# The place of six groups: a pass of two and then one of four, instead of four and then two

## The reference

```python
logits = (hf @ w_router + b_router)
top_val, top_idx = lax.top_k(logits, TOP_K)
gates = jax.nn.softmax(top_val, axis=-1)
# for each expert e and the tokens xb that chose it:
gu = xb @ w1[e] + b1[e]
gate, up = jnp.split(gu, 2, axis=-1)
gate = jnp.minimum(gate, 7.0); up = jnp.clip(up, -7.0, 7.0)
glu = gate * jax.nn.sigmoid(1.702 * gate)
y = ((up + 1.0) * glu) @ w2[e] + b2[e]
# each token sums its four y, weighted by its gates
```

## The kernel before

| loads | what | slots | free after |
|---|---|---|---|
| 56 to 63 | place 2, up chunks | 8 to 15 | earlier passes |
| 64 to 67 | place 19, down chunks | 0 to 3 | earlier passes |
| 68 to 71 | place 2, down chunks | 4 to 7 | earlier passes |
| 72 to 79 | place 20, up chunks | 8 to 15 | use of load 56 to 63 in up 6, one by one |
| 80 to 83 | place 21, up chunks 0 to 3 | 0 to 3 | down 4 |
| 84 to 87 | place 21, up chunks 4 to 7 | 4 to 7 | use of load 68 to 71 in down 6, one by one |
| 88 to 91 | place 20, down chunks | 8 to 11 | up 7 |

## Time and profile before

### The profile page before, as it was taken

How to read it: one execution, slowest core, us unless ns; L and a number is a source line. 1 busy time by engine, 2 the same in 40 slices (tenths; PEclk the granted TensorE clock), 3 DMA queues, 4 the chain that set the end, 5 groups by cost and what they waited for, 6 DMA issues and landing times.

```text
span 2083.2 us, 36376 instructions
## 1 busy us (share of the span) xinstructions
PE 1999.2 (96%) x15871; PEld 900.5 (43%) x15871; DVE 630.7 (30%) x1256; ACT 404.9 (19%) x837; POOL 53.6 (3%) x54
## 2 busy tenths in 40 slices
PE   8999897999999999999999999879999999999998
PEld 4455444433443343443443433455444444444443
DVE  5979765211111111111111110143444444300002
ACT  3223402110111010111110110113333443300001
POOL 0000000000000000000000000030000000000000
PEclk9999997999999999999999999989999999999999
DMA  8753686999899999999999999960222112122201
GB/s 325 264 212 132 240 314 268 420 419 359 327 420 420 420 418 421 419 420 420 419 420 420 419 420 419 395 242 11 104 66 74 63 64 69 57 81 71 81 32 70
DMA packets 109169, 553.82 MB, mean 266 GB/s; under 512 B 14864, under 2 KB 26128, under 8 KB 59216
## 3 DMA queue, kind: packets, MB, share of 16 engines
q1 hardware_dynamic: 87392, 517.36, 61.7%
q10 hardware_dynamic: 14560, 17.29, 2.5%
q0 software_dynamic: 7056, 16.79, 2.2%
HBM read 532.91 MB, written 26.35 MB: 268 GB/s over the span
## 4 chain that ended last, share of the span: by engine, by line
PE 69%; DMA 14%; SPq 9%; DVE 5%; issue 1%; ACT 1%; POOL 0%; ACTq 0%; DVEq 0%; POOLq 0%
PE psum L880 19%; PE psum L1058 13%; PE psum L1065 11%; SPq L417 9%; PE psum L888 8%; DMA arena<-in_w 6%; PE psum L556 4%; DMA ring<-in_w 3%; PE psum L1016 3%; PE psum L1128 3%; DMA ring<-in_dot_slabs 1%; PE psum L874 1%; DMA arena<-in_mod_slabs 1%; DMA ring<-in_mod_slabs 1%; PE psum L1106 1%
## 5 line engine op out<-in xcount | busy, mean ns | idle before, releaser
L880 PE MATMUL psum<-arena,ring 128*32 128x512 f32 x4096 | 451.7, 595 | 12.3 <-DMA arena<-in_w 11.8
L1058 PE MATMUL psum<-h_t,ring 128*128 128x512 f32 x640 | 278.6, 592 | 0.2 <-ACT arena L1432 0.2
L880 PEld LDWEIGHTS psum<-arena,ring 128*32 128x32 f32 x4096 | 133.2, 110 | 326.5 <-issue 324.0
L888 PE MATMUL psum<-arena,h_t 128*32 128x256 f32 x3840 | 213.8, 380 | 5.4 <-DMA arena<-in_w 4.6
L1957 DVE TENSOR_SCALAR h_t<-psum 128x512 f32<-128x512 f32 (+2 forms) x33 | 27.9, 845 | 608.2 <-PE psum L880 608.2
L1359 ACT ACTIVATE ring<-psum,mods,gain 128x64 f32<-128x64 f32 (+2 forms) x264 | 85.8, 430 | 641.9 <-PE psum L866 641.9
L1058 PEld LDWEIGHTS psum<-h_t,ring 128*128 128x128 f32 x640 | 120.4, 190 | 146.4 <-issue 145.9
L888 PEld LDWEIGHTS psum<-arena,h_t 128*32 128x32 f32 x3840 | 123.5, 110 | 87.5 <-DMA arena<-in_w 7.5
L880 PE MATMUL psum<-ring 128*32 128x512 f32 x1344 | 149.0, 593 | 7.8 <-DMA ring<-in_w 7.8
L556 PE MATMUL psum<-h_t,ring 128*128 128x512 f32 x256 | 118.8, 619 | 2.6 <-ACT h_t L1179 2.6
L1065 PE MATMUL psum<-h_t,ring 128*128 128x512 f32 x256 | 112.6, 592 | 1.4 <-ACT work L1243 1.4
(11 more groups left out here) (436 smaller groups left out, 1726.0 us busy)
## 6 DMA issues: line engine op xcount, KB each, us to landing
arena<-in_w SPq DMA_DIRECT2D x288, 1024.0 KB, 27.8
ring<-in_w SPq DMA_DIRECT2D x96, 1024.0 KB, 29.3
ring<-in_dot_slabs SPq DMA_DIRECT2D x40, 512.0 KB, 5.7
ring<-in_turn_slabs SPq DMA_DIRECT2D x40, 512.0 KB, 3.3
ring<-in_merge_slabs SPq DMA_DIRECT2D x32, 512.0 KB, 3.3
ring<-in_mod_slabs SPq DMA_DIRECT2D x6, 2048.0 KB, 13.2
ring<-in_proj_slabs SPq DMA_DIRECT2D x24, 512.0 KB, 4.1
y_rows<-arena SPq DMA_DIRECT2D x3, 3584.0 KB, 19.0
```

What stands on the lines that cost most here:

```text
L880: mm = pe.matmul(psum[32 * j:32 * j + 32, g, :], x_e[:, c * tokens + g * TG:c * tokens + g * TG + TG], slot[s][:, j * S:(j + 1) * S], star ...
L888: mm = pe.matmul(psum[32 * j:32 * j + 32, 6 + g // 2, (g % 2) * 256:(g % 2) * 256 + 256], h_e[:, g * 256 + half * P + 32 * c:g * 256 + hal ...
L1058: mm = pe.matmul(psum[:, bank, :], ring[:, s, k, :], h_t[:, k, :], start=(k == 0), stop=(k == KT - 1))
```

## The change

The list of passes is written differently. A place of up to four groups is one pass, as before. A larger one is first a pass with what is over four groups, and then one of four. Only place 2 has more than four groups, so pass 5 now has two groups and pass 6 four. Everything that is computed from `PASSES` follows: the first group of each pass, the table by which tokens find their rows, and `AT_GROUP`, by which the tokens of a pass of two groups lie in rows 64 to 127 of the gathered tile. The plan of loads, slots and counts is the same in every entry, since both passes use all 12 chunks in either order.

```diff
-PASSES = [(w, at, min(4, GROUPS_OF[w] - 4 * at)) for w in PLACES for at in range(-(-GROUPS_OF[w] // 4))]
+
+PASSES = [(w, at, n) for w in PLACES for at, n in enumerate([GROUPS_OF[w]] if GROUPS_OF[w] <= 4 else [GROUPS_OF[w] - 4, 4])]
```

## The result

The changed kernel takes 2089.16 us (median of 12 runs, 2085.11 to 2095.16), the kernel before 2083.21 (12 runs, 2077.55 to 2085.93). The ratio is 1.0029 with a 95% interval of 1.0019 to 1.0040. That is 6.0 us slower, 4.0 to 8.3. The forecast was 4.5 slower, with a range of 3.2 to 6.0.

A forecast was written before the change was run, and what follows sets the result against it. The weight stream was taken as the bound, restarting after the second hole: 3.8 us for load 91's later landing, 0.4 gather and 0.3 start sum to 4.5 slower, 2086.7; forecast range 3.2 to 6.0 us, whole range 2083.5 to 2090.

The forecast's parts named there:

- What bounds the stage: Mixture of experts: the weight stream bounds it; its end is the second hole's end plus a fixed amount of transfer.
- the second hole: Stretch from 544 to 552 with DMA share 0.02; load 84 has no slot until down 6 uses its first chunk.
- Steps 1 to 3: Up 5 and down 4 follow the loads, then transposes and bias; up 6 starts at 499.1, against 505.75 before.
- the gather's price: Pass 8's earlier gather may delay loads 66 and 67 by up to 0.8 us; half, 0.4, counted after step 2.
- Steps 4 to 6: Up 6 to down 6: down 6 starts at 551.0, load 84 is issued at 554.8, 2.4 us later.
- Behind load 84: Loads 84 to 87 issued 3.49 us apart, a store moved behind the hole; load 91 lands at 581.9, 3.8 later.
- the row of four loads behind load 87: Loads 88 to 91 follow load 87's landing at 570.4 at 2.48 us each, to 580.3, before the store's price.
- TensorE makes good its delay: After down 6 TensorE is 7.6 us late, the stream 4.5; the 3.1 between is gone by 676 through shorter waits.
- The clock: Rival, chance 0.04: TensorE's clock falls after waits from 468 to 497.5; end at 2114, or 2088.7 if only for 4 us.
- The spacing costs nothing: Rival, chance 0.12: the 3.49 us spacing behind the hole hides in slow first loads; only 2.4 us remain, 2084.6.
- The earlier refill counts: Rival, chance 0.04: load 72, issued 4.9 us earlier, keeps the queue from running dry before load 84; faster, 2081.1.
- The DMA price: Skill formula, 2.0 us fixed plus bytes at 436 GB/s: 4.4 us per load; the sum would be 3.8.

The follow-up runs named there:

- delays ahead and behind: Kernel before with nine idle TensorE products ahead of down 6: ratio 1.0029, 6.0 us slower; behind down 6: 0.9989, 2.3 us faster.
- the filled holes: Loads with free slots issued ahead of waiting ones; second hole only, against the kernel before: ratio 0.9957 with its passes, 0.9980 with the changed passes.
- the kernel with the spacing alone: Kernel before with two idle TensorE products ahead of each of the last three chunks of down 6: ratio 1.0016, 3.3 us slower.
- both holes filled: Loads reordered 80 to 83, 72 to 79, 88 to 95, 84 to 87, against the kernel before: ratio 0.9924 with its passes, 0.9938 with the changed passes.
- four and two: Passes 5 and 6 with four and then two groups, as in the kernel before; with the order of loads for both holes: ratio 0.9924, 2067.68 us.
- two and four: Passes 5 and 6 as in the changed kernel; with the order of loads for both holes: ratio 0.9938 against the kernel before, 2069.80 us.
- three and three: Changed kernel with place 2 in two passes of three groups: ratio 0.9998 against the kernel before; with the order for both holes 0.9919, 2065.47 us.
- the added stores: Kernel before with four more stores of 0.26 MB each issued right behind pass 6's own: ratio 1.0014, 2.9 us slower.

## Why the prediction was right

- **What bounds the stage.** Right. The delays ahead and behind and the filled holes show it from both sides: the stream, from the end of the second hole on.
- **Steps 1 to 3, up 6's start.** Up 6 started at 497.27 in the profile after, 146.4 us after load 16. The forecast's 499.1 is 145.3 on the same scale. Up 5 and down 4 went in the steps of the loads, as said:

```profile
480.81 1.92 PE L881 MATMUL psum<-arena,ring 128*32 128x512 f32 x16 [0.57 <-DMA arena<-in_w]
483.28 1.92 PE L881 MATMUL psum<-arena,ring 128*32 128x512 f32 x16 [0.55 <-DMA arena<-in_w]
...
493.75 1.93 PE L889 MATMUL psum<-arena,h_t 128*32 128x256 f32 x32 [1.18 <-DMA arena<-in_w]
...
497.27 27.69 PE L881 MATMUL psum<-arena,ring 128*32 128x512 f32 x256
```

  The 1.1 us are the last load of down 4, late with a wait of 1.18. I had counted half of the gather's price for it, 0.4. The gather was issued at 487.0, just ahead of it; that it is the cause is not shown.
- **Steps 4 to 6.** Right to 0.2 us. Down 6 starts at 549.12, 51.85 us after up 6 (the forecast has 51.9), and load 84 is issued at 552.98. The pair of profiles gives 3.5 us for the later issue, where the forecast had 2.4 and 0.4 for the gather. Part of that is the profile of before: in the seven kernels with its order of passes load 84 comes 198.6 to 200.9 us after load 16, 199.5 in the mean with the delay of 7.9 taken off. In the three with two and four it is 202.3, so 2.8 us, which is the forecast's sum. There is some luck in that: on the same scale the forecast has 201.4, and the profile that it started from was itself 0.9 us short of its mean.
- **Behind load 84.** The forecast went from 555.2 to 582.6 for load 91 with everything counted, 27.4 us. Measured are 27.7 (552.98 to 580.7), and 25.7 before: 2.0 us where I had 1.7. The split was off. The store was taken at 0.8 and is 0.6 by its experiment. The spacing was taken at 0.6 to 0.9 and is some 1.5, by its experiment and the correction assumed there. The term that I under-sized is the row of four loads behind load 87. They took 12.4 us (568.2 to 580.7), with the store between, and not 11.5. Before, the same four took 11.2 (566.9 to 578.1), so 1.2 of the 2.0 us lie in this row and 0.8 ahead of it; how they divide between the spacing and the store stays open. Nor did load 87 start on an empty queue, as the forecast says: load 86 landed 1.5 us after load 87 was issued. From load 16 to the landing of load 91 the shift is 5.5 us, and 5.8 at the last load, so it is found again there.
- **TensorE makes good its delay.** Right. Its waits for loads from 580 on were 21.9 us and are 19.0, where the forecast had 3.1 less. From 660 to 676 they are 0.5, and were 3.9:

```profile
PE psum L881 <- DMA arena<-in_w: 8.3, 12, 1.0
PE psum L881 <- DMA ring<-in_w: 6.8, 8, 1.9
PE psum L889 <- DMA arena<-in_w: 3.9, 6, 1.2
```

- **The clock.** It stayed at 1.00, the level of 2.4 GHz, while TensorE followed the loads for 31 us, busy for 25.4 of them:

```profile
465.00:496.00 31.00, 25.39 (x287) 9.13 (x285) 3.37 (x5) 3.99 (x11) 1.21 (x1) 1.00 1.01 420
```

  The Trainium skill says in "TensorE: Matmul & The Clock Gate", section "HAM oscillation — how this bites in real kernels", that TensorE can fall back to the slow clock at each wait of this kind. That did not come about here, with waits of 0.6 to 1.2 us, most of them between bursts of 1.9.
- **The spacing costs nothing.** This rival is wrong, as the forecast thought: 2.5 us in the kernel with the spacing alone, or 1.5 with the correction that I assume there.
- **The earlier refill counts.** Load 72 was issued 3.8 us earlier in the stage (150.2 us after load 16, not 154.1), and nothing of it reached load 84, with the share at 0.04 from 544 to 552. It does not count with both holes filled either: there load 79 landed 185.6 us after load 16 with four and two, and 185.9 with two and four.
- **The DMA price.** By the formula of the Trainium skill in "DMA: Bandwidth & Descriptors", section "Anatomy of one DMA — SWDGE (gpsimd) path", about 2.0 us fixed plus the bytes at 436 GB/s, a load is an estimate of 4.4 us. That was again below all rows: load 87 took 4.9, and load 84, on an empty queue, 5.6.

The size: 4.5 was said, 5.8 is the stage's difference in the pair of profiles, 6.0 the ratio's. By the means of all profiles the part up to load 84 is 2.8 us and the part behind it 2.3 to 2.5, 5.1 to 5.3 in all. So the sum was short by under a microsecond, and the rest is within what runs of one kernel differ. The shift of 6.0 lies at the very edge of the stated 3.2 to 6.0, and the median of 2089.16 is beyond the forecast's own 2088.2, though inside the whole range (to 2090): of that, 1.0 us is the median of before, 2083.21 over 12 runs and 2082.2 over the first three. The upper end of 6.0 was also added up wrong. The terms named for it (0.3 more for the load, 0.8 for the gather, 1.6 for the start, on 3.8) make 6.5.

## What to carry to other kernels

A stream of loads that is full at both ends can still have a hole, and where the queue runs dry in it, only the last hole sets the time: see when the queue is refilled, and by which work. Where one set of buffers is used by two passes, the second pass frees them, so it should start early and be the smaller one, or loads whose buffers are free should be issued ahead of those that wait. Then look again, since the stream can stop at the next load that waits. Here that last change, a list of 24 numbers, was worth 16 us by the runs (14 in the stage), and the order of the passes 6.

## What was not expected

- Executions differ outside the stage as well: the 12 runs of the kernel before spread over 8.4 us. The time from the last issue of a load to the end of the program, in which all the kernels do the same, was 756.8 us in the profile of three and three and 763.4 in that of the added stores. The windows taken of it show no cause, and it stays open.
- A load on an empty queue landed 4.6 to 7.2 us after its issue (load 72 in the kernel with the spacing, load 84 with three and three). In the changed kernel the loads behind load 87 then landed 2.8 to 3.6 us apart, for a time, and not 2.5.
- Filled holes do not let the queue run deep again. With both filled, loads issued after 586 still went out as late as 9.3 us before they landed, and from 582 to 1330 the stream still did not stop (share 1.02).
